# Sums of squares of the second block's head norms: two fp32r products of high and low parts in place of one fp32 product

## The chip, the cores and the metric

The kernel runs on one core of one Trainium2 chip. The metric is the device time of one execution in microseconds (us); the time of a kernel is the median of several executions.

## The reference, cut to what matters

Two transformer blocks are computed in fp32 for 256 tokens of width 2048. The change lies in the attention mixer of the second block, where 16 meta tokens are put ahead, so that there are 272 rows. The projection `h @ w_in` gives 16 query heads and 8 key heads of 128 features each, and each of these 24 heads is normalised by the root of the mean of its squares before the rotary turn:

```python
def rmsnorm_2(x, w):
    xf = x.astype(jnp.float32)
    y = xf * lax.rsqrt(jnp.mean(xf * xf, axis=-1, keepdims=True) + NORM_EPS)
    return (y * w.astype(jnp.float32)).astype(x.dtype)
...
    proj = h @ w_in
...
    q = apply_axial_rope(rmsnorm_2(q, q_norm), ang_row, ang_col)
    k = apply_axial_rope(rmsnorm_2(k, k_norm), ang_row, ang_col)
```

## The kernel before, in words

All weights stream from memory in units of 128 x 1024 numbers. SP's queue loads a unit into `raw` (8 buffers). ACT writes its high part `whi` in the type fp32r (`split`, L696), DVE writes the low part `wlo = raw - whi` (L1392), each in a ring of 4 buffers. The activations were split the same way into `ahi` and `alo`. TensorE (PE) makes three fp32r products in place of one fp32 product (`features`, L2241): high by high, high by low, low by high. A unit with 272 tokens has 2 row tiles times 4 column tiles times 3 products, that is 24 matmuls of 128x272.

The order on every engine is written out by hand, as a loop over trips and units. Beside unit j of a trip, ACT and DVE split the unit j + 3 (`LEAD`). A trip of the stage "aqk" is 8 units, the last of which ends four output tiles, that is four heads; ACT copies them from the PSUM banks 0 to 3 into `qk2` (L1097). There are six such trips; trips 2 to 5 are the body of a hardware loop (`Fori`), trips 0 and 1 are written out. The stage "av" (two trips) follows with the values, then the attention itself (`attend`), whose first score matmul (L2560) waits until all 24 heads are done (`qk_done`).

The norm of the four heads of a trip goes on beside the next trip, one head for two units. Head p of a trip belongs to the units 2p and 2p + 1:

- ACT, before the split beside the even unit: `Square` of the head into `sq2[:, p % 2]` (L1108).
- PE, behind the even unit: one fp32 matmul of the 128x128 matrix `ones` with `sq2` into bank 4 or 5 (L2532), which gives every partition the sum over the 128 features. It appears in the trace as two records.
- ACT, behind the split beside the even unit: `Sqrt` of the sum into `rs2` (L1115).
- DVE, behind its split beside the even unit (`qk_norm`): the reciprocal of `rs2` in place (L1853), then `n2` = head x gain x reciprocal (L1858).
- POOL: `nc2 = n2 * cos` (L2842). SP's queue: four small DMAs that write `n2` with halves exchanged into `turned2` (L615).
- DVE, behind its split beside the odd unit (`qk_rotate`), for the head before: `turned2 * sin` (L1865) and the sum with `nc2` (L1869).

The norms of the heads of the last "aqk" trip so go on beside trip 0 of "av", and the last head is turned in trip 1 of "av", ahead of `attend`.

Of the kernel before, what the change touches and what calls it, by code (L numbers as in the profile page):

```python
# [17 lines left out]
F32 = mybir.dt.float32  # L18
F32R = mybir.dt.float32r
ALU = mybir.AluOpType  # L20
ACT = mybir.ActivationFunctionType
AX = mybir.AxisListType

P = 128
# [4 lines left out]
T2 = TB + TM  # L29
# [15 lines left out]
AT_HEADS, AT_KV, AT_HD = 16, 8, 128  # L45
# [14 lines left out]
TRIPS, UNITS, CHUNKS, U0, C0 = {}, {}, {}, {}, {}  # L60
# [23 lines left out]
def at(const, trip, per_trip):  # L84

    return trip * per_trip + const


def under(const, trip, per_trip, bound):

    return isinstance(trip, int) and trip * per_trip + const < bound
# [36 lines left out]
def two_blocks_kernel(nc, A, out):  # L128

    ctx = ExitStack()  # L130
    with ctx:
        place_at = [(nc.sbuf_base + 31) // 32 * 32]

        def sb(name, shape, dt=F32, at_=None):

            size = int(np.prod(shape[1:])) * 4
            off = place_at[0] if at_ is None else at_
            t = nc.alloc_sbuf_tensor_at(name, shape, dt, offset=off)
            if at_ is None:
                place_at[0] = off + (size + 31) // 32 * 32  # L140
            return t

        def sem(name):
            return ctx.enter_context(nc.semaphore(name))
# [7 lines left out]
        eps = lam[:, 5:6]  # L152
# [9 lines left out]
        ones = sb("ones", [P, P])  # L162
# [15 lines left out]
        R2 = place_at[0] + (128 - place_at[0]) % 256  # L178
# [11 lines left out]
        def in_turns(ap):  # L190

            return ap.rearrange("p (h c) -> p c h", h=2)

        def halves(ap):

            return ap.rearrange("p (h c) -> p h c", h=2)

        def untwined(ap):

            return ap.rearrange("p (c h) -> p h c", h=2)  # L200
# [9 lines left out]
        def ha(t, k, c0, n):  # L210
# [50 lines left out]
        pT2 = sb("pT2", [P, 2, 2, T2], F32R, at_=R2 + 4 * (24 * T2 + 3 * 1024 + KD * T2 + 6 * T2))  # L261
        pT2_low = [sb("pT2_low0", [P, 2, T2], F32R, at_=R2 + 4 * (24 * T2 + 3 * 1024 + KD * T2 + 10 * T2)),
                   sb("pT2_low1", [P, 2, T2], F32R, at_=tmp_at)]
        qmeta = sb("qmeta", [P, AT_HEADS * TM], F32, at_=msq_at)
        vt2_at = R2 + 4 * (24 * T2 + 3 * 1024 + KD * T2 + 12 * T2 + 2 * 3 * AT_HEADS)
        pad_at = vt2_at + 4 * (2 * 4 * T2 + 2 * T2)
# [28 lines left out]
        bank = ctx.enter_context(nc.psum_tensor("bank", [P, 8, 512], F32))  # L295
# [27 lines left out]
        def chunk_of(ph, j):  # L323

            if ph == "kvb":
                return 0, j == 0, j == 3
            if ph == "oabc":
                return 3 * (j // 8) + min(j % 8 // 2, 2), j % 8 in (0, 2, 4), j % 8 in (1, 3, 7)
            if ph == "down":
                return j // 24, j % 24 == 0, j % 24 == 23  # L330
            if ph == "lr":
                return 0, True, True
            return j // 8, j % 8 == 0, j % 8 == 7
# [83 lines left out]
        tap2, tap1, gelu_done, ff_prod, ffhi_ready = map(  # L417
            sem, "tap2 tap1 gelu_done ff_prod ffhi_ready".split())

        const_in, x_terms = sem("const_in"), sem("x_terms")  # L420
        qk_sq, qk_sum, qk_root, qk_rstd, qk_normed, qk_cos, qk_sin, qk_done = map(
            sem, "qk_sq qk_sum qk_root qk_rstd qk_normed qk_cos qk_sin qk_done".split())
        qk_turned = [sem("qk_turned0"), sem("qk_turned1")]
# [31 lines left out]
        def x_updates(b, tt, c1):  # L455

            return N_XU[b] + max(n + 1 for n, (row, _, end) in enumerate(X_PIECES[b]) if row == tt and end <= c1)
# [228 lines left out]
        def _(act):  # L686
# [414 lines left out]
            def qk_norm(i, j):  # L1101

                p, late = divmod(j, 2)
                if not late:
                    act.wait_ge(acc_free, at(4 * C0["aqk"] + p - 3, i, 4))
                    if not under(p - 4, i, 4, 2):
                        act.wait_ge(qk_sum, at(p - 5, i, 4))
                    act.activation(sq2[:, p % 2:p % 2 + 1, :], qk2[:, bass.ds(i * 4 + (p - 4), 1), :], ACT.Square)\  # L1108
                       .then_inc(qk_sq, 1)

            def qk_late(i, j):
                p, late = divmod(j, 2)
                if not late:
                    act.wait_ge(qk_sum, at(p - 3, i, 4))
                    act.activation(rs2[:, p % 2, :], bank[:, 4 + p % 2, 0:T2], ACT.Sqrt, bias=eps, scale=1.0 / AT_HD)\  # L1115
                       .then_inc(qk_root, 1)

            qk_out = feature_out(qk2, T2, ACT.Copy)
# [262 lines left out]
        def _(dve):  # L1381
            def split(u, i=0, n=0):

                if not under(u, i, n, N_UNITS) and isinstance(i, int):
                    return
                dve.wait_ge(whi_ready, at(u + 1, i, n))
                if is_rank_unit(u, i, n):
                    dve.tensor_tensor(rank_columns(u, 1), rank_rows(u), rank_columns(u, 0).bitcast(F32), ALU.subtract)\
                       .then_inc(wlo_ready, 1)
                    return  # L1390
                c = unit_width(u, i, n)
                dve.tensor_tensor(wlo[:, u % RING, 0:c], raw[:, u % RAW, 0:c], whi[:, u % RING, 0:c].bitcast(F32),  # L1392
                                  ALU.subtract).then_inc(wlo_ready, 1)

            def trip(ph, i, read_out=None, before=None, after=None, split_before=0, held=0):
                n = UNITS[ph]
                for j in range(n):
                    if before:
                        before(i, j)
                    if split_before <= j < n - held:  # L1400
                        split(U0[ph] + j + LEAD, i, n)
                    chunk, _, ends = chunk_of(ph, j)
                    if ends and read_out:
                        read_out(i, chunk, U0[ph] + j, n)
                    if after:
                        after(i, j)
# [439 lines left out]
            def qk_norm(i, j):  # L1846
                p, odd = divmod(j, 2)
                if odd:
                    if not under(p - 5, i, 4, 0):
                        qk_rotate(p - 1, i)  # L1850
                    return
                dve.wait_ge(qk_root, at(p - 3, i, 4))
                dve.reciprocal(rs2[:, p % 2, :], rs2[:, p % 2, :]).then_inc(qk_rstd, 1)  # L1853
                dve.wait_ge(qk_rstd, at(p - 3, i, 4))
                if not under(p - 4, i, 4, 2):
                    dve.wait_ge(qk_turned[p % 2], at(64 * (p // 2 - 2), i, 128))
                    dve.wait_ge(qk_cos, at(p - 5, i, 4))
                dve.scalar_tensor_tensor(n2[:, p % 2:p % 2 + 1, :], qk2[:, bass.ds(i * 4 + (p - 4), 1), :],  # L1858
                                         qkgain[:, bass.ds(i * 4 + (p - 4), 1)], rs2[:, p % 2:p % 2 + 1, :],
                                         ALU.mult, ALU.mult).then_inc(qk_normed, 1)  # L1860

            def qk_rotate(p, i):
                head = qk2[:, bass.ds(i * 4 + (p - 4), 1), :]
                dve.wait_ge(qk_turned[p % 2], at(64 * (p // 2 - 1), i, 128))
                dve.tensor_tensor(head, turned2[:, p % 2:p % 2 + 1, :], sin[:, :].rearrange("p (o t) -> p o t", o=1),  # L1865
                                  ALU.mult).then_inc(qk_sin, 1)
                dve.wait_ge(qk_sin, at(p - 3, i, 4))
                dve.wait_ge(qk_cos, at(p - 3, i, 4))
                dve.tensor_tensor(head, head, nc2[:, p % 2:p % 2 + 1, :], ALU.add).then_inc(qk_done, 1)  # L1869
# [60 lines left out]

            trip("aqk", 0, after=later_lo(2))
            dve.wait_ge(const_in, 32)
            trip("aqk", 1, after=qk_norm)
            with dve.Fori(2, TRIPS["aqk"]) as i:
                trip("aqk", i, after=qk_norm)
            trip("av", 0, after=lambda i, j: qk_norm(TRIPS["aqk"], j))
            def rotated(i, j):

                if j:
                    attend(j - 1)  # L1940
                    return
                qk_rotate(3, TRIPS["aqk"])
                dve.wait_ge(qk_done, 24)
                dve.tensor_copy(qmeta[:, :].rearrange("p (h t) -> p h t", t=TM), qk2[:, 0:AT_HEADS, TB:T2]).then_inc(qk_done, 1)
# [258 lines left out]
        def _(pe):  # L2203
# [254 lines left out]
            for j in range(UNITS["kvb"]):  # L2458
# [6 lines left out]
                for k in range(nk):  # L2465
                    for wp, ap in PASSES:
                        mm = pe.matmul(bank[:, 0, 0:TB], w[wp][:, k, 0:P], in_turns(ha((ahi, alo)[ap], k0 + k, 0, TB)),
                                       start=begins and k == 0 and (wp, ap) == (0, 0), stop=ends and k == nk - 1 and wp == 1)
# [54 lines left out]
            def qk_norm(i, j):  # L2523


                p, odd = divmod(j, 2)
                if odd:
                    return
                pe.wait_ge(qk_sq, at(p - 3, i, 4))
                if not under(p - 4, i, 4, 2):  # L2530
                    pe.wait_ge(qk_root, at(p - 5, i, 4))
                pe.matmul(bank[:, 4 + p % 2, 0:T2], ones[:, :], sq2[:, p % 2, :], start=True, stop=True).then_inc(qk_sum, 1)  # L2532

            TOK = ((0, P), (P, P), (TB, TM))

# [262 lines left out]
            for i in range(TRIPS["gout"]):  # L2798
                for j in range(UNITS["gout"]):
# [4 lines left out]
                    for tt in range(2):  # L2804
# [7 lines left out]
                        for k in range(nk):  # L2812
                            for wp, ap in PASSES:
                                mm = pe.matmul(bank[:, b, :], gated(ap, k0 + k)[:, tt * P:(tt + 1) * P], in_turns(w[wp][:, k, :]),  # L2814
                                               start=begins and k == 0 and (wp, ap) == (0, 0),
                                               stop=ends and k == nk - 1 and wp == 1)
# [74 lines left out]
```

## Time and profile before

| | |
|---|---|
| median of 3 executions | 2201.83 us (2200.68 to 2202.99) |
| the profiled execution, its own time | 2203.46 us |
| its span in the trace | 2201.7 us |
| PE busy | 2173.4 us, 99% of the span |
| DVE busy | 1444.9 us, 66% |
| ACT busy | 1193.2 us, 54% |
| POOL busy | 191.6 us, 9% |
| mean granted TensorE clock, of full | 0.997 |

A busy share is an average over all stages. Matmuls are pipelined and each record goes on until its result is out, so that a busy PE is read from the distance between the starts of two matmuls. "Idle before" an instruction is the time its engine stood still, with the instruction that ended it. The chain that ended last is followed back from the end of the program: at each step to what released it, or to the instruction before it on its engine.

### The profile page before, as it was taken

How to read it: one execution, taken by the hardware profiler on the slowest of the kernel's cores; microseconds unless marked ns; L12 is line 12 of the kernel's file. 1: busy time of each engine (PE TensorE's matmuls, PEld its weight loads, DVE VectorE, ACT ScalarE, POOL GpSimd, SP SyncE). 2: the span in 40 equal slices, each digit the busy share in tenths (PEclk: the TensorE clock that was granted, in tenths of full speed). 3: DMA queues.
4: the chain of work that ended last, by engine and by line, in shares of the span. 5: the costliest groups of instructions: out<-in, count | busy, mean ns of one | idle time of the engine just before them, and what ended most of it. 6: DMA issues, size and time to landing. Idle time of an engine off the chain costs nothing.

```text
span 2201.7 us, 43774 instructions
## 1 busy us (share of the span) xinstructions
PE 2173.4 (99%) x17103; PEld 2082.3 (95%) x17103; DVE 1444.9 (66%) x1913; ACT 1193.2 (54%) x1813; POOL 191.6 (9%) x146
## 2 busy tenths in 40 slices
PE   9999999999999999999999999999999999999998
PEld 9898999999889999999988889999999999999987
DVE  5556644448568777777855556998676565567754
ACT  5455644445455555454544445555666565676553
POOL 0000000000002121221200000221000000012110
PEclk9999999999999999999999999999999999999999
DMA  8645466656655666656566665565345547555454
GB/s 288 193 153 163 144 205 195 197 161 223 230 162 187 207 192 190 207 180 211 180 213 205 205 202 177 186 195 181 117 123 181 183 137 233 170 161 145 140 200 149
DMA packets 258873, 405.69 MB, mean 184 GB/s; under 512 B 16655, under 2 KB 115852, under 8 KB 257708
## 3 DMA queue, kind: packets, MB, share of 16 engines
q1 hardware_dynamic: 257060, 396.87, 57.3%
q10 hardware_dynamic: 1688, 7.07, 0.9%
q8 instruction: 88, 1.44, 0.3%
q14 instruction: 37, 0.30, 0.0%
HBM read 396.32 MB, written 4.22 MB: 182 GB/s over the span
## 4 chain that ended last, share of the span: by engine, by line
PE 92%; DVE 4%; ACT 3%; issue 1%; DMA 0%; SPq 0%; DVEq 0%; ACTq 0%
PE bank L2241 65%; PE bank L2346 14%; PE bank L2814 3%; PE bank L2256 2%; DVE wlo L1392 1%; PE bank L2560 1%; ACT whi L696 1%; PE bank L2782 1%; PE bank L2738 1%; DVE rs L1853 1%; PE bank L2598 1%; PE bank L2281 1%; DVE xtok L1546 0%; PE bank L2532 0%; DMA xtok<-in_x 0%
## 5 line engine op out<-in xcount | busy, mean ns | idle before, releaser
L1392 DVE TENSOR_TENSOR wlo<-raw,whi 128x1024 fp32r<-128x1024 f32 (+1 forms) x748 | 927.4, 1250 | 614.6 <-ACT whi L696 610.6
L2241 PE MATMUL bank<-ahi,whi 128*128 128x256 f32 (+1 forms) x4224 | 1183.0, 280 | 7.0 <-DVE alo L1611 3.7
L2241 PE MATMUL bank<-ahi,wlo 128*128 128x256 f32 (+1 forms) x4224 | 1168.4, 277 | 0.0
L2241 PE MATMUL bank<-alo,whi 128*128 128x256 f32 (+1 forms) x4224 | 1168.3, 277 | 0.0
L696 ACT ACTIVATE whi<-raw 128x1024 fp32r<-128x1024 f32 (+1 forms) x748 | 771.4, 1039 | 644.9 <-PE bank L2241 435.4
L2241 PEld LDWEIGHTS bank<-ahi,whi 128*128 128x128 f32 x4224 | 808.4, 191 | 14.1 <-issue 8.0
L2241 PEld LDWEIGHTS bank<-alo,whi 128*128 128x128 f32 x4224 | 808.4, 191 | 1.3 <-issue 0.2
L2241 PEld LDWEIGHTS bank<-ahi,wlo 128*128 128x128 f32 x4224 | 808.3, 191 | 0.0
L2346 PE MATMUL bank<-whi,ghi 128*128 128x512 f32 x352 | 133.5, 379 | 0.3 <-DVE wlo L1392 0.3
L2346 PE MATMUL bank<-whi,glo 128*128 128x512 f32 x352 | 133.4, 379 | 0.0
L2346 PE MATMUL bank<-wlo,ghi 128*128 128x512 f32 x352 | 133.4, 379 | 0.0
L2832 POOL CAST ghi<-pr 128x256 f32 x44 | 40.0, 909 | 737.1 <-DVE pr L1826 737.1
L1819 DVE SCALAR_TENSOR_TENSOR cv<-bank,par,cv 128x255 f32<-128x255 f32 (+1 forms) x176 | 78.7, 478 | 11.9 <-DVE cv L1819 1.5
L2346 PEld LDWEIGHTS bank<-whi,ghi 128*128 128x128 f32 x352 | 66.5, 189 | 10.1 <-DVE wlo L1392 0.7
L2346 PEld LDWEIGHTS bank<-wlo,ghi 128*128 128x128 f32 x352 | 66.5, 189 | 9.4
L2346 PEld LDWEIGHTS bank<-whi,glo 128*128 128x128 f32 x352 | 66.5, 189 | 9.4
L2825 POOL TENSOR_TENSOR glo<-pr,ghi 128x256 f32 x44 | 65.5, 1489 | 7.2 <-POOL ghi L2832 7.2
L1073 ACT ACTIVATE cv<-bank,par 128x256 f32<-128x256 f32 x88 | 42.5, 564 | 38.4 <-DVE bank L1813 38.4
L2241 PE MATMUL bank<-yhi,whi 128*128 128x256 f32 x192 | 52.8, 275 | 0.0
L2241 PE MATMUL bank<-ylo,whi 128*128 128x256 f32 x192 | 52.8, 275 | 0.0
L2241 PE MATMUL bank<-yhi,wlo 128*128 128x256 f32 x192 | 52.8, 275 | 0.0
L2842 POOL TENSOR_TENSOR nc<-n,cos 128x272 f32<-128x272 f32 x24 | 40.3, 1679 | 111.1 <-DVE n L1858 111.1
(389 smaller groups left out, 2223.9 us busy)
## 6 DMA issues: line engine op xcount, KB each, us to landing
raw<-in_w_up SPq DMA_DIRECT2D x176, 512.0 KB, 4.7
raw<-in_w_in SPq DMA_DIRECT2D x156, 512.0 KB, 4.4
raw<-in_attn_w_in SPq DMA_DIRECT2D x96, 512.0 KB, 4.2
raw<-in_gla_w_in SPq DMA_DIRECT2D x96, 512.0 KB, 3.8
raw<-in_w_down SPq DMA_DIRECT2D x80, 512.0 KB, 4.5
raw<-in_w_out SPq DMA_DIRECT2D x32, 512.0 KB, 4.7
raw<-in_attn_w_out SPq DMA_DIRECT2D x32, 512.0 KB, 3.8
raw<-in_gla_w_out SPq DMA_DIRECT2D x32, 512.0 KB, 4.5
```

The source lines that it names most:

```text
L696: act.activation(whi[:, u % RING, 0:c], raw[:, u % RAW, 0:c], ACT.Copy).then_inc(whi_ready, 1)
L1073: act.activation(cv[:, t, :], bank[:, 4 * chunk + t, TB:2 * TB], ACT.Identity, bias=par[:, bass.ds(i * 4 + (PAR["conv_b"] + r), 1)], scale ...
L1392: dve.tensor_tensor(wlo[:, u % RING, 0:c], raw[:, u % RAW, 0:c], whi[:, u % RING, 0:c].bitcast(F32), ALU.subtract).then_inc(wlo_ready, 1)
L1819: dve.scalar_tensor_tensor(cv[:, t, back:TB], bank[:, 4 * chunk + t, TB:2 * TB - back], tap, cv[:, t, back:TB], ALU.mult, ALU.add).then_in ...
L1853: dve.reciprocal(rs2[:, p % 2, :], rs2[:, p % 2, :]).then_inc(qk_rstd, 1)
L2241: mm = pe.matmul(bank[:, base + t, 0:T], w[wp][:, k, col:col + P], in_turns(rhs(ap, k0 + k)), start=begins and k == 0 and (wp, ap) == (0, ...
L2256: mm = pe.matmul(bank[:, first_bank + tt, 0:cols[1] - cols[0]], ha((ahi, alo)[ap], k0 + k, tt * P, P), in_turns(w[wp][:, k, cols[0]:cols[1]]),
L2346: mm = pe.matmul(bank[:, row_bank(b, c, tt), :], tokens_of, in_turns(w[wp][:, k, :]), start=begins and k == 0 and (wp, ap) == (0, 0), stop ...
L2814: mm = pe.matmul(bank[:, b, :], gated(ap, k0 + k)[:, tt * P:(tt + 1) * P], in_turns(w[wp][:, k, :]), start=begins and k == 0 and (wp, ap) ...
L2825: pool.tensor_tensor(dst, whole, high.bitcast(F32), ALU.subtract).then_inc(done, 1)
L2832: pool.tensor_copy(ghi[:, bass.ds(i * 4 + t, 1), :], pr[:, t % 2:t % 2 + 1, :]).then_inc(ffhi_ready, 1)
L2842: pool.tensor_tensor(nc2[:, n % 2, :], n2[:, n % 2, :], cos[:, :], ALU.mult).then_inc(qk_cos, 1)
```

## The change

For each of the 24 heads the squares are split, too. ACT, behind its `Square`, copies `sq2` into `sq2hi` in the type fp32r. DVE gets a new function `squares_low` that stands ahead of its split beside the even unit and writes `sq2lo = sq2 - sq2hi`. PE waits for `sq_low` in place of `qk_sq` and makes two fp32r products of `ones` (read as fp32r), one with `sq2hi` and one with `sq2lo`. Both read their operand with its two halves in turns, as the products of `features` do, so ACT's `Sqrt` puts the columns back in order when it reads the bank. `sq2hi` and `sq2lo` lie where the values `v2` are written later. Lines of `kernel.py` behind the new ones move by 2 to 14.

```diff
+        sq2hi = sb("sq2hi", [P, 2, T2], F32R, at_=R2 + 4 * 24 * T2)
+        sq2lo = sb("sq2lo", [P, 2, T2], F32R, at_=R2 + 4 * (24 * T2 + 2 * T2))
...
-        const_in, x_terms = sem("const_in"), sem("x_terms")
+        const_in, x_terms, sq_low = sem("const_in"), sem("x_terms"), sem("sq_low")
...
                     act.activation(sq2[:, p % 2:p % 2 + 1, :], qk2[:, bass.ds(i * 4 + (p - 4), 1), :], ACT.Square)\
                        .then_inc(qk_sq, 1)
+                    act.wait_ge(qk_sq, at(2 * (p - 3) - 1, i, 8))
+                    act.activation(sq2hi[:, p % 2, :], sq2[:, p % 2, :], ACT.Copy).then_inc(qk_sq, 1)
...
-                    act.activation(rs2[:, p % 2, :], bank[:, 4 + p % 2, 0:T2], ACT.Sqrt, bias=eps, scale=1.0 / AT_HD)\
+                    act.activation(halves(rs2[:, p % 2, :]), untwined(bank[:, 4 + p % 2, 0:T2]), ACT.Sqrt, bias=eps, scale=1.0 / AT_HD)\
                        .then_inc(qk_root, 1)
...
+            def squares_low(i, j):
+
+                p, odd = divmod(j, 2)
+                if not odd:
+                    dve.wait_ge(qk_sq, at(2 * (p - 3), i, 8))
+                    dve.tensor_tensor(sq2lo[:, p % 2, :], sq2[:, p % 2, :], sq2hi[:, p % 2, :].bitcast(F32), ALU.subtract)\
+                       .then_inc(sq_low, 1)
...
-            trip("aqk", 1, after=qk_norm)
+            trip("aqk", 1, before=squares_low, after=qk_norm)
             with dve.Fori(2, TRIPS["aqk"]) as i:
-                trip("aqk", i, after=qk_norm)
-            trip("av", 0, after=lambda i, j: qk_norm(TRIPS["aqk"], j))
+                trip("aqk", i, before=squares_low, after=qk_norm)
+            trip("av", 0, before=lambda i, j: squares_low(TRIPS["aqk"], j), after=lambda i, j: qk_norm(TRIPS["aqk"], j))
...
-                pe.wait_ge(qk_sq, at(p - 3, i, 4))
+                pe.wait_ge(sq_low, at(p - 3, i, 4))
                 if not under(p - 4, i, 4, 2):
                     pe.wait_ge(qk_root, at(p - 5, i, 4))
-                pe.matmul(bank[:, 4 + p % 2, 0:T2], ones[:, :], sq2[:, p % 2, :], start=True, stop=True).then_inc(qk_sum, 1)
+                every = ones[:, :].bitcast(F32R)
+                pe.matmul(bank[:, 4 + p % 2, 0:T2], every, in_turns(sq2hi[:, p % 2, :]), start=True, stop=False)
+                pe.matmul(bank[:, 4 + p % 2, 0:T2], every, in_turns(sq2lo[:, p % 2, :]), start=False, stop=True).then_inc(qk_sum, 1)
```

How DVE's instructions stand in the second head of the loop's body, before the change (`rs` is `rs2`, `n` is `n2`, `nc` is `nc2`, `qk` is `qk2`, `sq` is `sq2`):

```order
L1392 TENSOR_TENSOR wlo<-raw,whi 128x1024 [waits whi_ready]
L1852 REGISTER_ALU
L1853 RECIPROCAL rs_130<-rs_130 128x272 [waits qk_root]
L1858 ISA [waits qk_cos,qk_turned1,qk_rstd]
L1858 SCALAR_TENSOR_TENSOR n_131<-qk_122,qkgain,rs_130 128x272
```

And now:

```order
L1870 REGISTER_ALU
L1871 TENSOR_TENSOR sq2lo<-sq_129,sq2hi 128x272 [waits qk_sq]
L1390 REGISTER_ALU
L1396 TENSOR_TENSOR wlo<-raw,whi 128x1024 [waits whi_ready]
L1856 REGISTER_ALU
L1857 RECIPROCAL rs_130<-rs_130 128x272 [waits qk_root]
L1862 ISA [waits qk_cos,qk_turned1,qk_rstd]
L1862 SCALAR_TENSOR_TENSOR n_131<-qk_122,qkgain,rs_130 128x272
```

The subtraction and one register instruction stand ahead of the split; nothing else has moved.

## Rows read from the trace of the kernel before

**Rows 1.** The page, busy time of each engine: busy us, share, instructions
```profile
PE 2173.4 (99%) x17103; PEld 2082.3 (95%) x17103; DVE 1444.9 (66%) x1913; ACT 1193.2 (54%) x1813; POOL 191.6 (9%) x146
```
**Rows 2.** Windows of the norm stage: us, busy per engine, PEclk, DMA share, GB/s
```profile
1400.53:1425.27 24.74, 24.74 (x209) 24.43 (x207) 23.65 (x26) 13.28 (x21) 6.72 (x4) 1.00 0.61 193
1425.27:1499.19 73.92, 73.92 (x617) 72.98 (x616) 70.85 (x74) 38.31 (x63) 20.14 (x12) 1.00 0.61 193
1499.19:1517.10 17.91, 17.91 (x151) 17.68 (x150) 17.70 (x19) 9.03 (x14) 5.05 (x3) 1.00 0.63 200
```
**Rows 3.** Chain that ended last, in order of time, 1470 to 1526: start, us, what
```profile
1471.73 0.46 PE bank L2532 x2
1472.19 5.56 PE bank L2241 x48
1477.75 0.47 PE bank L2532 x2
...
1479.74 1.22 DVE wlo L1392
```
**Rows 4.** Timeline of DVE, one head in the loop, 1429 to 1437
```profile
1429.05 1.00 DVE L1865 TENSOR_TENSOR qk<-turned,sin 128x272 f32 x1
1430.09 0.44 DVE L1869 TENSOR_TENSOR qk<-qk,nc 128x272 f32 x1
1430.45 1.22 DVE L1392 TENSOR_TENSOR wlo<-raw,whi 128x1024 fp32r<-128x1024 f32 x1
1431.59 1.84 DVE L1853 RECIPROCAL rs<-rs 128x272 f32<-128x272 f32 x1
...
1436.19 0.44 DVE L1869 TENSOR_TENSOR qk<-qk,nc 128x272 f32 x1
```
**Rows 5.** Timeline of DVE, trips written out: heads 2 and 24
```profile
1382.47 1.85 DVE L1853 RECIPROCAL rs<-rs 128x272 f32<-128x272 f32 x1 [0.79 <-ACT rs L1115]
...
1517.10 1.85 DVE L1853 RECIPROCAL rs<-rs 128x272 f32<-128x272 f32 x1
...
1523.79 0.44 DVE L1865 TENSOR_TENSOR qk<-turned,sin 128x272 f32<-128x272 f32 x1 [0.63 <-DMA turned<-n]
1524.27 0.44 DVE L1869 TENSOR_TENSOR qk<-qk,nc 128x272 f32<-128x272 f32 x1
```
**Rows 6.** Timeline of PE around one sum, 1429.3 to 1430.2
```profile
1429.32 0.28 PE L2241 MATMUL bank<-ahi,wlo 128*128 128x272 f32 x1
1429.44 0.62 PE L2532 MATMUL bank<-sq,ones 128*128 128x272 f32 x2
```
**Rows 7.** Timeline of ACT, the same head
```profile
1425.41 0.42 ACT L1108 ACTIVATE sq<-qk 128x272 f32 x1
1426.86 1.06 ACT L696 ACTIVATE whi<-raw 128x1024 fp32r<-128x1024 f32 x1 [1.03 <-PE bank L2241]
1430.10 0.49 ACT L1115 ACTIVATE rs<-bank,lam 128x272 f32<-128x272 f32 x1 [2.18 <-PE bank L2532]
```
**Rows 8.** Timeline of POOL, the product with the cosines of the same head
```profile
1428.08 1.67 POOL L2842 TENSOR_TENSOR nc<-n,cos 128x272 f32<-128x272 f32 x1 [4.68 <-DVE n L1858]
```
**Rows 9.** Timeline of PE after waits for DVE
```profile
1353.98 0.35 PE L2241 MATMUL bank<-ahi,whi 128*128 128x272 f32 x1 [0.35 <-DVE alo L1611]
...
1524.76 1.18 PE L2560 MATMUL bank<-qk 128*128 128x272 f32 x4 [2.11 <-DVE qk L1869]
...
1526.92 0.43 PE L2241 MATMUL bank<-ahi,wlo 128*128 128x272 f32 x1
1527.15 0.43 PE L2241 MATMUL bank<-ahi,whi 128*128 128x272 f32 x1
```
**Rows 10.** Windows behind waits of PE, columns as in rows 2
```profile
1526.00:1529.00 3.00, 3.00 (x16) 2.88 (x14) 1.17 (x4) 2.41 (x7) 0.00 (x0) 0.50 0.92 305
630.00:636.00 6.00, 4.25 (x35) 3.85 (x35) 4.58 (x11) 2.82 (x6) 0.00 (x0) 1.00 0.22 72
1786.00:1792.00 6.00, 4.60 (x26) 4.40 (x27) 4.47 (x9) 4.68 (x8) 0.00 (x0) 0.73 0.00 0
```

## The prediction

> **What bounds the kernel now.** I first read the busy times: PE is busy for 99% of the span, DVE for 66% [rows 1]. Over the whole program a PE instruction saved is time saved. But a share of the whole says nothing of one stage, so I next cut the stage of the change into windows [rows 2]. There PE is busy without a break at full clock, and so nearly is DVE: 70.85 of 73.92 us, and 17.70 of 17.91. The two engines are level, and what the change takes from PE it gives to DVE.
>
> The chain of waits says who is ahead [rows 3]. Up to 1477.75 it runs over PE: 5.56 us of 48 products for two units and 0.46 us for the sum, 6.02 us for a head. From 1479.74 on it runs over DVE, from its split to the end of the stage.
>
> DVE's own time for a head comes from its timeline. In the loop the sum L1869 starts at 1430.09 and again at 1436.19, 6.10 us later [rows 4]; with a longer pause in the first head of each trip, 12 heads take 73.92 us [rows 2], 6.16 each. In the trips written out it is 17.91 / 3 = 5.97 us. So DVE falls back behind PE by 0.1 us a head in the loop, and the 24th head is done at 1524.27 + 0.44 = 1524.71 [rows 5], while PE has stood still for 2.11 us before the first score matmul, which waits for it [rows 9]. **The end of this stage is set by DVE, not by PE.**
>
> **Where the new subtraction lands.** PE starts a sum at 1429.44 [rows 6]. DVE comes to its split of the same step only at 1430.45 [rows 4], and the subtraction stands ahead of that split. Before, PE needed only ACT's square, which had been there since 1425.83 [rows 7]. Now it needs something that DVE does 1 us after PE arrives. Hence the change adds a wait of PE for DVE in every head, and behind the waiting matmul stand the 48 products of the next two units.
>
> **The change part by part.**
>
> *PE.* The fp32 sum costs 0.46 us of PE's time [rows 3]. Two fp32r products of 128x272 cost two start distances of such products, 5.56 / 48 = 0.116 us, thus 0.23 us. PE saves 0.23 us x 24 = 5.5 us of work and needs 5.79 us a head. As PE then waits for DVE, none of this reaches the end except through the latency of the sum, below.
>
> *ACT.* One copy of 128x272 more per head, about the 0.42 us of the square beside it [rows 7]. It stands ahead of a split before which ACT waits 1.03 us for PE, and 2.18 us more before the root [rows 7]. The copy is over some 3 us before DVE asks for it. Cost zero; if that cover were gone, 0.42 us a head. Reading the bank with its halves untwined: nothing at best, and at most 0.07 us a head, by which the root (0.49) is longer than the square (0.42), the nearest rows.
>
> *DVE.* Its subtraction has the shape of L1869, which lasts 0.44 us and lets the next instruction start after 0.36 [rows 4]. The Trainium skill, VectorE: DVE Perf Modes (the comparison of its cycle formulas with measured times), has (N + 151) / 0.96 for an fp32 `tensor_tensor`, 441 ns for 272 columns. As a duration the trace agrees; as a price for each instruction in a row it would make 0.08 us a head too much, 1.8 us in all, and here the start distance decides. Could POOL block the subtraction? Beside POOL's product the multiplication L1865 takes 1.00 us, without it 0.44 [rows 4, 5]. POOL is done at 1428.08 + 1.67 = 1429.75 [rows 8], 0.7 us before the place of the subtraction, so I add nothing; the overlap would cost 0.56 us.
>
> *The loop through the engines.* From the start of the subtraction to the start of the reciprocal there are two paths. On DVE: 0.36 + the split's 1.14 [rows 4] = 1.50 us. Through PE and ACT: 0.44 for the subtraction, 0.05 until PE starts (1524.71 to 1524.76), up to 0.12 with what a first product after a wait takes longer (0.35 against 0.28) [rows 6, 9], 0.116 + 0.28 for the two products [rows 6], 0.04 and ACT's root of 0.49, 0.05 to DVE: 1.47 to 1.54, and 1.61 if the untwining costs its 0.07. The paths are level. Before, the same piece took 1.14. So a head grows by 0.36 to 0.47, and I take 0.39, near the lower end, where both paths lie without a surcharge.
>
> *The sum.* The first root comes as before, the second 0.25 us earlier because a sum is shorter. From the reciprocal of the second head (1382.47) to that of the 24th (1517.10) [rows 5] there are 22 distances: 22 x 0.39 = 8.6 us. Three of them were 6.02 us, set by PE ((1400.53 - 1382.47) / 3), where DVE alone needs 5.97: minus 0.15. Together 8.6 - 0.25 - 0.15 = +8.2 us for the end of the last head.
>
> *What PE does there.* The reciprocal of the 24th head starts at R; the score matmul is free at R + 7.61 (1524.71 - 1517.10). PE now starts the last sum at R - 0.98 and has 0.23 + 3 units x 2.78 = 8.57 us of work, until R + 7.6. The wait of 2.11 us shrinks to almost nothing. After that wait the granted clock was 0.50 from 1526 to 1529, the lower level of 1.2 GHz [rows 10], products started 0.23 us apart in place of 0.116 [rows 9], and 12 of them cost some 1.4 us. Without the wait I count this as won: -1.5 us, with what lies around. Behind it nothing else of the change is felt.
>
> Total **+8.2 - 1.5 = +6.7 us**: the profiled execution would go from 2203.46 to 2210.2. It stood 1.6 us above the median of the executions shown; on the median the forecast is 2201.83 + 6.7 = **2208.5 us**, slower by 0.3%.
>
> **Rivals.**
>
> *A, PE is the bound as its 99% says.* Then 24 x 0.23 = 5.5 us are won: 2196.3 us, and more by the wait of 2.11 us if DVE kept up. It decides as soon as DVE's time for a head is under PE's new 5.79 us. For it speaks the chain before 1477; against it that DVE needs 5.97 to 6.16 already without the subtraction. Chance 0.04.
>
> *B, much of the subtraction vanishes in DVE's pauses.* DVE is idle for 73.92 - 70.85 = 3.1 us over 12 heads in the loop [rows 2], 4.1 over 16. If a longer order of work filled them: 6.7 - 4.1 = +2.6, 2204.4 us, no change. Against it: the pauses lie between the reciprocal and the instruction that needs its result, and the subtraction is not there. Chance 0.10, with half of it for what else could make the sum smaller.
>
> *C, PE's clock falls in the waits.* Each head now holds a wait of 5.97 + 0.39 - 5.79 = 0.57 us, in the loop 0.7 or more. The wait of 2.11 us was followed by 3 us at half clock. From 630 to 636 PE stood still for 6.00 - 4.25 = 1.75 us and kept a granted clock of 1.00, from 1786 to 1792 for 1.40 us and got 0.73 [rows 10]. A fall costs 1.5 us, of which the wait of the next head takes back 0.7: 0.8 x 22 = 17 us more at worst, 2227. Here 0.7 us stand among 5.8 us of work, half of what either row holds. The Trainium skill, TensorE: Matmul & The Clock Gate (A second HAM failure mode: psum-queue depth-cycling), describes a kernel in which short idle times between groups of matmuls let the clock go to and fro; by that rule the change would be worse than its instructions. Chance 0.04.
>
> *D, the products are not made as fp32r.* If `ones` read as fp32r were still multiplied as fp32, a sum would take 0.92 us of PE and the path to the reciprocal 0.46 + 0.62 in place of 0.40, 0.68 more a head: 6.7 + 15 = 2223.5 us. Against it: L2241 multiplies tiles of the same type with one record each. Chance 0.02.
>
> **How the numbers follow.** The forecast has the chance 0.80. Its low end: 0.36 us a head (-0.7) and the longer pauses of four trips hidden (-1.0), +5.0. Its high end: 0.47 (+1.8), a register instruction before the subtraction that costs another 0.13 in 16 heads (+2.1), the clock at the end falls as before (+1.5), +12.1, of which not all come together. With some 1.2 us by which executions differ, 2205.6 to 2214.0. A measurement can tell about 0.2%, 4.4 us. Faster: 0.04 from A. Same: 0.12, B and the lower edge. Slower: 0.84.
>
> **What would show it.** Right: a wait before each sum, named as for DVE's subtraction, 0.6 to 0.9 us each, 13 us and more in all; DVE's heads 6.5 us apart in the loop and 6.4 outside; two records of 0.28 us for a sum; the wait before the first score matmul under 0.5 us and the clock behind it at 1.00; ACT's waits unchanged in kind. Wrong: PE without idle time in the stage (A), DVE's pauses gone and heads less than 6.3 us apart (B), a granted clock under 0.95 (C), sums of 0.39 us records (D).

## The result and the profile after

The changed kernel takes **2211.03 us** (median of 6 executions, 2210.43 to 2212.37), the kernel before, beside it, 2201.96 us. The ratio is 1.0043, 95% interval 1.0033 to 1.0053: 9.1 us slower, 0.4%. The forecast was 2208.5 us, with a range of 2205.6 to 2214.0. The profiled execution took 2211.57 us and its span 2209.8 us, 8.1 more than that of before.

The page of the changed kernel, busy times, beside [rows 1]:

```profile
PE 2171.2 (98%) x17103; PEld 2077.7 (94%) x17103; DVE 1453.8 (66%) x1937; ACT 1202.3 (54%) x1837; POOL 191.4 (9%) x146
```

PE is busy 2 us less, DVE 9 us more, in a program that is slower by about as much, though DVE is busy for only 66% of it. The windows of the stage show why, between the second reciprocal and the 24th, columns as in [rows 2]:

```profile
1382.16:1401.39 19.23, 18.17 (x153) 17.57 (x152) 18.97 (x21) 11.04 (x20) 5.04 (x3) 1.00 0.64 189
1401.39:1507.21 105.82, 96.91 (x803) 93.72 (x802) 101.33 (x113) 57.18 (x97) 26.86 (x16) 1.00 0.58 180
1507.21:1526.37 19.16, 18.18 (x153) 17.57 (x152) 18.95 (x23) 9.71 (x16) 5.04 (x3) 1.00 0.60 188
```

Before, PE had no idle time here. Now the second number of each row falls short of the first: 144.21 - 133.26 = 11 us of idle PE, while DVE works nearly without a pause. The 22 distances between reciprocals take 144.21 us in place of 1517.10 - 1382.47 = 134.63.

Who makes PE wait: the waits of the stage, "engine line <- who", us in total, times, longest:

```profile
POOL nc L2856 <- DVE n L1862: 119.4, 24, 8.0
ACT rs L1119 <- PE bank L2546: 55.8, 24, 3.0
ACT whi L698 <- PE bank L2253: 12.1, 19, 1.5
PE bank L2545 <- DVE sq2lo L1871: 10.9, 22, 0.8
```

The last row is new. The loop through the engines is best followed in one head of the loop. DVE's timeline, as [rows 4]:

```profile
1439.69 0.43 DVE L1871 TENSOR_TENSOR sq2lo<-sq,sq2hi 128x272 fp32r<-128x272 f32 x1
1440.05 1.22 DVE L1396 TENSOR_TENSOR wlo<-raw,whi 128x1024 fp32r<-128x1024 f32 x1
1441.24 1.85 DVE L1857 RECIPROCAL rs<-rs 128x272 f32<-128x272 f32 x1
```

PE's, as [rows 6]:

```profile
1440.18 0.38 PE L2545 MATMUL bank<-sq2hi,ones 128*128 128x272 f32 x1 [0.47 <-DVE sq2lo L1871]
1440.40 0.28 PE L2546 MATMUL bank<-sq2lo,ones 128*128 128x272 f32 x1
```

and ACT's:

```profile
1440.72 0.49 ACT L1119 ACTIVATE rs<-bank,lam 128x272 f32<-128x272 f32 x1 [2.69 <-PE bank L2546]
```

Subtraction at 1439.69, done at 1440.12; PE starts at 1440.18, its second product 0.22 us later; the root at 1440.72, done at 1441.21; the reciprocal at 1441.24. That is 1.55 us. DVE itself was through with the split at 1440.05 + 1.14 = 1441.19 and waited 0.05 us. So it is in 14 of the 22 heads; in the other eight, the first two of each trip of the loop, PE starts 0.13 to 0.14 us after the end of the subtraction in place of 0.06, and the path lasts 1.61 to 1.63 us. Reciprocals are 6.52 us apart in the loop (1441.24 - 1434.72), where they were 6.10.

At the end of the stage, PE's timeline as in [rows 9] and the clock as in [rows 10]:

```profile
1534.58 1.18 PE L2574 MATMUL bank<-qk 128*128 128x272 f32 x4 [0.43 <-DVE qk L1881]
```
```profile
1536.00:1539.00 3.00, 3.00 (x27) 2.87 (x26) 1.18 (x3) 2.59 (x7) 0.00 (x0) 1.00 0.75 256
```

The wait of 2.11 us has become 0.43, and the three microseconds behind it, which had a granted clock of 0.50 before (the lower level, 1.2 GHz), now have 1.00 (2.4 GHz): 27 records in place of 16. The first score matmul starts 9.82 us later than before; but DVE's third reciprocal in the attention behind it (L1910, L1898 before) stands at 1558.24 against 1550.07, only 8.17 us later. So 1.65 us come back in between.

### The profile page after: what moved, and what is told of

Same layout as the page of the kernel before. It is cut to its first block, busy times and chain, and to the rows that moved or that the text cites. A ratio compares the mean times of both kernels' runs of the same rounds, so it can differ in the third digit from the quotient of the medians.

```text
span 2209.8 us, 43850 instructions
## 1 busy us (share of the span) xinstructions
PE 2171.2 (98%) x17103; PEld 2077.7 (94%) x17103; DVE 1453.8 (66%) x1937; ACT 1202.3 (54%) x1837; POOL 191.4 (9%) x146
## 4 chain that ended last, share of the span: by engine, by line
PE 87%; DVE 8%; ACT 3%; issue 1%; DMA 1%; DVEq 0%; SPq 0%; ACTq 0%
PE bank L2253 61%; PE bank L2358 14%; PE bank L2828 3%; DVE wlo L1396 3%; PE bank L2268 2%; DVE rs L1857 2%; DVE qk L1877 1%; PE bank L2574 1%; ACT whi L698 1%; PE bank L2796 1%; PE bank L2752 1%; PE bank L2612 1%; DVE xtok L1550 0%; PE bank L2293 0%; DVE sq2lo L1871 0%
```

## The experiments

The theory: in this stage DVE's order of work sets the end, each head lasting as long as the longer of DVE's own path and the path subtraction, PE, ACT's root, reciprocal. Its rivals: PE is the bound; or only the place of the wait costs. Each kernel was timed beside the kernel before, which took 2201.96 us beside the changed kernel, 2202.03 beside e1 to e4 and 2201.87 beside e5 to e8.

| kernel | median, us | ratio to before, 95% interval |
|---|---|---|
| before | 2201.87 to 2202.03 | |
| after | 2211.03 | 1.0043 (1.0033 to 1.0053) |
| e1, no low part | 2202.28 | 1.0002 (0.9992 to 1.0011) |
| e2, fp32 sum, subtraction kept | 2215.84 | 1.0066 (1.0049 to 1.0082) |
| e3, subtraction half a head earlier | 2208.23 | 1.0028 (1.0016 to 1.0039) |
| e4, subtraction twice | 2216.88 | 1.0070 (1.0053 to 1.0087) |
| e5, subtraction on POOL | 2211.42 | 1.0051 (1.0035 to 1.0066) |
| e6, before, later product on POOL | 2199.53 | 0.9993 (0.9984 to 1.0002) |
| e7, after, later product on POOL | 2198.08 | 0.9985 (0.9976 to 0.9994) |
| e8, both on POOL | 2194.08 | 0.9969 (0.9958 to 0.9980) |

**e1: PE's saving without DVE's load.** The kernel leaves out the low part of the squares and counts the high part twice; only its time is of use.

The same is done to the other two trips with `squares_low`.

```diff
-            trip("aqk", 1, before=squares_low, after=qk_norm)
+            trip("aqk", 1, after=qk_norm)
...
-                pe.wait_ge(sq_low, at(p - 3, i, 4))
+                pe.wait_ge(qk_sq, at(2 * (p - 3), i, 8))
...
-                pe.matmul(bank[:, 4 + p % 2, 0:T2], every, in_turns(sq2lo[:, p % 2, :]), start=False, stop=True).then_inc(qk_sum, 1)
+                pe.matmul(bank[:, 4 + p % 2, 0:T2], every, in_turns(sq2hi[:, p % 2, :]), start=False, stop=True).then_inc(qk_sum, 1)
```

> Leaves out the low part of the squares: DVE does not subtract, PE waits for ACT's copy and multiplies the high part twice, so PE's saving of 0.23 us a head stays and DVE's load is that of before. DVE sets the stage's end: its heads are 5.97 to 6.16 us apart again, PE no longer waits at the sums, the wait before the first score matmul grows from 2.1 us to about 7.5 (2.1 + 24 x 0.23), the clock falls behind it again: 2201 to 2203 us, that is nothing gained although PE does 5.5 us less. Rival, PE is the bound: 2196.4 us.

It took 2202.28 us, level with before. PE does 5.5 us less and nothing comes of it; rival A, by which PE is the bound, falls. Two waits of the stage:

```profile
PE bank L2574 <- DVE qk L1881: 3.6, 1, 3.6
```
```profile
PEld bank L2253 <- DVE wlo L1396: 1.4, 5, 0.5
```

The wait before the first score matmul was 3.6 us, not 7.5. The score matmul could start 1.8 us earlier (1522.98 against 1524.76). And PE, now ahead, did not keep all of its lead: from 1458 on its starts show 2.7 us of delays, one in each head, of which the waits named above, for DVE's splits of the weights, are 1.4. This execution also came to the stage 0.6 us earlier, so 7.6 - 1.8 - 2.7 + 0.6 = 3.7. The granted clock fell to 0.50 about 1 us before this wait ended and stayed there for 5.4 us behind it (1522.98 to 1528.40), longer than the 3 us of before. Of the 1.8 us only 0.7 are left in the spans (2201.0 against 2201.7). Two windows of it:

```profile
1519.00:1524.00 5.00, 1.36 (x5) 0.97 (x5) 4.83 (x8) 0.01 (x1) 1.04 (x1) 0.79 0.57 182
1524.00:1527.00 3.00, 3.00 (x13) 2.29 (x12) 1.18 (x3) 1.89 (x6) 0.00 (x0) 0.50 0.88 279
```

**e2: the longer sum put back, with the root that reads its bank in plain order; everything else kept.**

```diff
-                pe.matmul(bank[:, 4 + p % 2, 0:T2], every, in_turns(sq2hi[:, p % 2, :]), start=True, stop=False)
-                pe.matmul(bank[:, 4 + p % 2, 0:T2], every, in_turns(sq2lo[:, p % 2, :]), start=False, stop=True).then_inc(qk_sum, 1)
+                pe.matmul(bank[:, 4 + p % 2, 0:T2], ones[:, :], sq2[:, p % 2, :], start=True, stop=True).then_inc(qk_sum, 1)
```

> The copy, the subtraction and PE's wait for it stay, but the sum is the fp32 product of before. If the path subtraction, PE, ACT's root, reciprocal sets a head: it becomes 0.44 + 0.12 + 0.62 + 0.04 + 0.49 + 0.05 = 1.76 us in place of some 1.57, +0.2 us a head, 22 heads +4.4: about 2215 us. Rival, DVE's own load alone sets a head: PE needs 6.02 us a head, less than DVE's 6.5, and the time stays at 2211 us.

2215.84 us, 4.8 more than the changed kernel, as the loop through the engines has it. DVE's timeline in one head outside the loop:

```profile
1529.16 0.43 DVE L1871 TENSOR_TENSOR sq2lo<-sq,sq2hi 128x272 fp32r<-128x272 f32 x1
1529.51 1.22 DVE L1396 TENSOR_TENSOR wlo<-raw,whi 128x1024 fp32r<-128x1024 f32 x1
1530.93 1.85 DVE L1857 RECIPROCAL rs<-rs 128x272 f32<-128x272 f32 x1 [0.20 <-ACT rs L1119]
```

1.77 us from subtraction to reciprocal, and DVE waits for the root before it. So once DVE's subtraction is on the way to the sum, the sum's length counts, and the fp32r products are worth 0.2 us a head (reciprocals are 6.61 us apart here, 6.39 in the changed kernel). The change made the sum shorter and critical in one stroke.

**e3: the same instructions, the subtraction earlier.**

```diff
                 if odd:
+                    if not (isinstance(i, int) and i == TRIPS["aqk"] and j == 7):
+                        squares_low(i, j + 1)
                     if not under(p - 5, i, 4, 0):
                         qk_rotate(p - 1, i)
                     return
...
-            trip("aqk", 1, before=squares_low, after=qk_norm)
+            squares_low(1, 0)
+            trip("aqk", 1, after=qk_norm)
```

> The same instructions, but DVE subtracts a head's squares half a head earlier, behind its split beside the odd unit, so that the sum finds it done. Load theory: the subtraction still costs its 0.36 us a head; the 0.07 us a head of the path through the engines goes (-1.6), PE now waits for the split in place of the sum and some 4.9 us before the first score matmul, so the clock falls again (+1.5): 2210 to 2211.5 us. Rival, the place of the wait is the cost: then nearly all of the 9.1 us comes back, about 2202 us.

2208.23 us, 2.8 less than the changed kernel and below the 2210 to 2211.5 that had been expected. Two thirds of the loss remain. DVE:

```profile
1429.17 1.22 DVE L1396 TENSOR_TENSOR wlo<-raw,whi 128x1024 fp32r<-128x1024 f32 x1
1430.30 1.00 DVE L1873 TENSOR_TENSOR sq2lo<-sq,sq2hi 128x272 fp32r<-128x272 f32 x1
1431.23 0.43 DVE L1879 TENSOR_TENSOR qk<-turned,sin 128x272 f32 x1
1431.69 0.44 DVE L1883 TENSOR_TENSOR qk<-qk,nc 128x272 f32 x1
```

The edit moves PE's wait less than was meant. In the next head the subtraction starts at 1443.20 and is done at 1444.20, and PE's sum starts at 1444.25:

```profile
PE bank L2548 <- DVE sq2lo L1873: 8.4, 20, 0.6
```

So this run does not show what the changed kernel would take without waits of PE. What it shows is that DVE's own order is enough to set a head: in the 22 heads DVE waits for no root, save 0.2 us once, and its reciprocals are still 6.45 us apart in the loop (1439.63 to 1446.08), 0.07 less than in the changed kernel.

Two things more differ from what was expected. The subtraction now lasts 1.00 us and the multiplication behind it 0.43, where that had lasted 1.00: whichever comes behind the split while POOL multiplies is the one held up. And the wait before the first score matmul was only 1.16 us, with a granted clock of 1.00 behind it, so that the 1.5 us stayed won.

**e4: the subtraction twice.**

```diff
                    dve.tensor_tensor(sq2lo[:, p % 2, :], sq2[:, p % 2, :], sq2hi[:, p % 2, :].bitcast(F32), ALU.subtract)\
                       .then_inc(sq_low, 1)
+                    dve.tensor_tensor(sq2lo_too[:, p % 2, :], sq2[:, p % 2, :], sq2hi[:, p % 2, :].bitcast(F32), ALU.subtract)
```

> DVE makes the subtraction a second time into a tile that nobody reads, behind the first and its signal. If DVE's own path and the path through the engines are level, only what DVE's path is then longer counts: 0.70 + 1.14 = 1.84 us against 1.57, +0.27 us a head, +6 us: 2217 us. If DVE alone set a head: +0.35 x 22 = +7.7, 2218.7. If the path through PE and ACT set it with room to spare: 2211 us.

2216.88 us, 5.9 more than the changed kernel: 0.27 us a head for an instruction of 0.35. The other 0.08 us is, on the average of the heads, what DVE's path had in hand against the loop through PE and ACT (0.05 in 14 of them, more in the eight with the longer path). DVE no longer waits for the root:

```profile
1529.66 0.43 DVE L1872 TENSOR_TENSOR sq2lo<-sq,sq2hi 128x272 fp32r<-128x272 f32 x1
1530.02 0.43 DVE L1874 TENSOR_TENSOR sq2lo_too<-sq,sq2hi 128x272 fp32r<-128x272 f32 x1
1530.37 1.22 DVE L1397 TENSOR_TENSOR wlo<-raw,whi 128x1024 fp32r<-128x1024 f32 x1
1531.50 1.84 DVE L1858 RECIPROCAL rs<-rs 128x272 f32<-128x272 f32 x1
```

**e5: the subtraction on POOL, which is busy for a quarter of the stage.** POOL makes it behind its product:

```diff
             for n in range(24):
                 pool.wait_ge(qk_normed, n + 1)
                 if n >= 2:
                     pool.wait_ge(qk_done, n - 1)
                 pool.tensor_tensor(nc2[:, n % 2, :], n2[:, n % 2, :], cos[:, :], ALU.mult).then_inc(qk_cos, 1)
+                if n < 23:
+                    squares_low(n + 1)
```

> The subtraction of the low part goes from DVE to POOL, behind POOL's product for the head before. It should fall beside DVE's reciprocal, which reads one tile only, so that DVE is not held up. Load theory: DVE's heads are 5.97 to 6.16 us apart as before the change, PE waits several us before the first score matmul: about 2202 us, all of the 9 us back and nothing gained. Rival: POOL's and DVE's instructions with two inputs hold each other up, some 0.56 us a head as with L1865: about 2214 us.

Here the expectation of 2202 us failed, and its rival of 2214 was nearer: 2211.42 us, nothing gained. DVE and POOL in one head:

```profile
1437.64 1.22 DVE L1396 TENSOR_TENSOR wlo<-raw,whi 128x1024 fp32r<-128x1024 f32 x1
1438.78 1.01 DVE L1877 TENSOR_TENSOR qk<-turned,sin 128x272 f32 x1
1439.82 0.88 DVE L1881 TENSOR_TENSOR qk<-qk,nc 128x272 f32 x1
```
```profile
1437.81 1.68 POOL L2862 TENSOR_TENSOR nc<-n,cos 128x272 f32<-128x272 f32 x1 [3.95 <-DVE n L1862]
1439.45 0.95 POOL L2854 TENSOR_TENSOR sq2lo<-sq,sq2hi 128x272 fp32r<-128x272 f32 x1
```

POOL's product starts beside the split and ends at 1439.49, and its subtraction follows at once, not beside the reciprocal. DVE's L1881 now lasts 0.88 us in place of 0.44: what POOL takes over from DVE, DVE loses in waiting. The two engines' instructions with two inputs seem to go one after the other. The Trainium skill, SBUF — State Buffer (SBUF: two separate sides), says that a VectorE operation with two SBUF inputs and a GpSimd operation that reads SBUF take one shared pair of ports in turns, each for a whole instruction. With that the trace agrees, here and in e3: POOL's product, 0.77 us long where nothing holds it (e6), ends 0.71 us after DVE's split gives way to the next instruction (1438.78).

**e6, e7: POOL's product moved beside the reciprocal.** In the kernel before (e6) and in the changed one (e7):

```diff
             for n in range(24):
                 pool.wait_ge(qk_normed, n + 1)
+                if n < 23:
+                    pool.wait_ge(qk_root, n + 2)
```

> The kernel before with one wait more on POOL: its product with the cosines starts only when the root of the next head is ready, beside DVE's reciprocal. If POOL's product is what makes L1865 last 1.00 us in place of 0.44, DVE needs 0.56 us less a head, 5.4 to 5.6, and PE's 6.02 us set the stage: the last head is done 2.1 us earlier and the clock does not fall: 2198.4 us. Rival, L1865 is slow for its own sake: 2202 us.

> The changed kernel with the same late product. DVE's heads go from 6.39 and 6.52 us to about 5.85 and 6.0, near PE's 5.79: the last head is done some 12 us earlier than in the changed kernel, 3 us earlier than before the change, and the clock stays: 2197 us. If PE were the bound of the changed kernel: 2211.

e6 took 2199.53 us, 2.3 less than before with an interval that just includes no change; 2198.4 had been expected. The 24th reciprocal came 2.8 us earlier (1514.30), the score matmul only 1.7, as DVE waited 1.7 us for the last exchange of halves. What the trace shows of a head is clear. POOL and DVE in one head:

```profile
1436.16 0.77 POOL L2844 TENSOR_TENSOR nc<-n,cos 128x272 f32<-128x272 f32 x1 [5.25 <-ACT rs L1115]
```
```profile
1436.06 1.85 DVE L1853 RECIPROCAL rs<-rs 128x272 f32<-128x272 f32 x1 [0.39 <-ACT rs L1115]
1438.50 1.22 DVE L1392 TENSOR_TENSOR wlo<-raw,whi 128x1024 fp32r<-128x1024 f32 x1
1439.64 0.44 DVE L1865 TENSOR_TENSOR qk<-turned,sin 128x272 f32 x1
```

The product lasts 0.77 us in place of 1.67 and DVE's multiplication with the sines 0.44 in place of 1.00; DVE now waits for the root, that is for PE. e7 took 2198.08 us, where 2197 had been expected: one wait on POOL takes 13 us off the changed kernel, and PE's waits for the subtraction go from 10.9 us to 0.8. DVE's order of work, not PE's load, was its bound.

**e8: both on POOL**, with the late product, the subtraction for the head after next behind it:

```diff
+            squares_low(0)
+            squares_low(1)
             for n in range(24):
                 pool.wait_ge(qk_normed, n + 1)
+                if n < 23:
+                    pool.wait_ge(qk_root, n + 2)
...
+                if n < 22:
+                    squares_low(n + 2)
```

> Both on POOL: the late product, then the subtraction for the head after next. DVE alone would need 5.4 to 5.6 us a head and PE 5.79, so PE is the bound and its saving of 0.23 us a head counts at last: 2193.5 us. Rival: the subtraction on POOL comes when DVE works on two inputs and holds it up by part of 0.6 us a head: 2196 to 2199.

**2194.08 us, 7.8 us less than before and 17 less than the changed kernel.** POOL:

```profile
1435.00 0.77 POOL L2865 TENSOR_TENSOR nc<-n,cos 128x272 f32<-128x272 f32 x1 [3.36 <-issue]
1436.67 0.77 POOL L2854 TENSOR_TENSOR sq2lo<-sq,sq2hi 128x272 fp32r<-128x272 f32 x1 [0.90 <-ACT sq2hi L1113]
```

A window of 129 us that ends with its last reciprocal, columns as in [rows 2]:

```profile
1381.40:1510.40 129.00, 129.00 (x1114) 128.98 (x1113) 123.72 (x134) 78.57 (x132) 34.56 (x44) 1.00 0.66 204
```

PE has no idle time left, DVE has some. The subtraction is not free for DVE, either. In most heads it reaches into the instruction behind the reciprocal, which lasts 0.69 us (median of the 24) in place of 0.50:

```profile
1436.97 0.76 DVE L1862 SCALAR_TENSOR_TENSOR n<-qk,qkgain,rs 128x272 f32<-128x272 f32 x1 [0.17 <-DVE rs L1857]
```

That DVE can afford here, since PE sets the head. Against e6, which has the fp32 sums, e8 is 5.4 us faster: the 24 x 0.23 = 5.5 us that the change takes from PE arrive in full once DVE is out of the way.

## Why the prediction was right, point by point

- **DVE sets the end of the stage, not PE with its 99%.** Shown by e1 (PE's saving alone gives nothing) and e7 (relief for DVE gives 13 us).
- **The subtraction lands 1 us behind PE's arrival, so PE waits in every head.** 22 waits, 10.9 us in all, where 13 us and more had been forecast. They were expected at 0.6 to 0.9 us and read 0.3 to 0.8, because idle time is counted only from the end of the last product's record, 0.16 us after PE could have started the next.
- **A head grows by 0.39 us: the term that was too small.** The 22 distances grew by 144.21 - 134.63 = 9.6 us, where 8.6 - 0.15 = 8.4 had been added up: some 1.1 us more. DVE's side was right: 0.36 for the subtraction. The path through the engines measured 1.55 us in 14 heads and 1.61 to 1.63 in eight, against "1.47 to 1.54". What was short is "0.116 + 0.28 for the two products": behind a wait the second product starts 0.22 us after the first, not 0.116. In the eight heads PE also starts 0.07 us later behind the subtraction; why was not tried. So the loop, not DVE's own order, sets a head, by 0.05 us or more; e4 shows the same from the other side.
- **+8.2 us for the last head.** The 24th reciprocal came 9.3 us later, the first score matmul 9.8 us. The last 0.55 us was not foreseen: from the start of DVE's L1862 to the landing of the last exchange of halves it took 5.33 us, before 4.79, and DVE waited 1.18 us for it, before 0.63 [rows 5]. In the chain of waits the transfer behind the last issue lasts 2.98 us in place of 1.87. Why was not tried.
- **The wait at the end shrinks and 1.5 us come back with the clock.** Wait 0.43 us, granted clock 1.00, and 1.65 us came back. In all 9.3 + 0.55 - 1.65 = 8.2 us, against 8.1 by the spans. The forecast of 6.7 lacked the 1.1 us of the term above and this 0.55. The medians differ by 9.1, because the profiled execution of before stood 1.5 us above its median and that of the changed kernel 0.5; that part of the miss is chance.
- **Costs of nothing.** ACT's copy (0.43 us) made nobody wait but DVE, once, for 1.7 us at the start of the stage. POOL's product, at no cost in the forecast, held up one subtraction of 24, that of the second head (1379.81, 1.00 us), ahead of the stretch that DVE sets; nothing came of it. The untwined root lasts 0.49 us as before. The register instructions cost DVE nothing that shows: the pauses before L1862 add up to 3.6 us as before.
- **Rivals.** A is out by e1. B (the subtraction hides in DVE's pauses) is out, as the pauses stayed. C (the clock falls in the waits) is out: the granted clock stayed at 1.00 through 22 waits, and the rule of the Trainium skill that was named for it (TensorE: Matmul & The Clock Gate, A second HAM failure mode: psum-queue depth-cycling) found no case here. D (no fp32r products) is out by the two single records of a sum.

## What to carry to other kernels

Before work is moved from the busiest engine to one that is idle a third of the time, cut the trace to the stage: an engine with a share of 66% in the whole was at 96% here, and decided. Check in the timeline where the new instruction stands in its engine's order against the moment at which its result is wanted, and follow the loop back to that engine. And an instruction of 0.44 us that lasts 1.00 beside another engine's work is a reserve: find it a neighbour that does not block it before adding anything.

## What the runs showed of the hardware that was not expected

- POOL's multiplication of 128x272 lasts 0.77 us beside DVE's reciprocal (e6) and 1.68 us when it starts beside a DVE subtraction of 128x1024 (e5). Moving the subtraction from DVE to POOL gained nothing where the two engines' instructions met (e5), and 4 us behind the late product (e8 against e7); moving the product away from DVE's split gained 13 us (e7).
- Behind a wait of PE of 2.11 us (before) the granted clock was 0.50 for 3 us (1526 to 1529), behind one of 3.6 (e1) for 5.4 us (1522.98 to 1528.40). Waits of 0.43 (after), 0.97 (e6) and 1.16 us (e3) at the same place were not.
- A pair of fp32r products behind a wait starts 0.22 us apart (the changed kernel), in a stream 0.11 to 0.116 (e1, e8).
